# Where the attention half of the even layer's output projection is computed

## The reference, cut to what matters

```python
def attn_delta_mixer(h, pos, w_in, conv_w, a_log, dt_bias, q_gain, k_gain, sinks, gdn_gain, w_out):
    ...
    y_a = sliding_window_attention(partial_rope(q, pos), partial_rope(k, pos), v, sinks)   # (1, 512, 512)
    ...
    o = gated_delta_rule(bq, bk, bv, beta, g)                                              # 4 heads of 128
    o = rms_norm(o, gdn_gain).astype(h.dtype) * jax.nn.silu(bz.reshape(head_shape))
    y_b = o.reshape(bsz, s, GDN_W)
    return jnp.concatenate([y_a, y_b], axis=-1) @ w_out                                    # (1024 -> 1024)

def step(state, inp):            # the recurrence inside gated_delta_rule, one chunk of tokens at a time
    u_c, w_c, a_c, qd_c, kd_c, gl_c = inp
    v_new = u_c - jnp.einsum('bhck,bhkv->bhcv', w_c, state)
    out = jnp.einsum('bhck,bhkv->bhcv', qd_c, state) + jnp.einsum('bhij,bhjv->bhiv', a_c, v_new)
    state = state * gl_c[..., None, None] + jnp.einsum('bhck,bhcv->bhkv', kd_c, v_new)
    return state, out

# layer: x = x + attn_delta_mixer(rms_norm(x), ...);  x = x + hierarchical_moe(rms_norm(x), ...)
```

## Time and profile before

| | |
|---|---|
| median of 3 runs | 1832.97 us (1831.81 to 1833.87) |
| the profiled execution, its own time | 1832.23 us |
| its span | 1830.4 us |
| PE busy | 1754.8 us (96%), 9209 instructions |
| DVE busy | 679.5 us (37%) |
| ACT busy | 452.4 us (25%) |
| POOL busy | 241.1 us (13%) |
| mean granted TensorE clock | 0.981 |

### The profile page before, as it was taken

How to read it: one execution, slowest core, us unless ns; L and a number is a source line. 1 busy time by engine, 2 the same in 40 slices (tenths; PEclk the granted TensorE clock), 3 DMA queues, 4 the chain that set the end, 5 groups by cost and what they waited for, 6 DMA issues and landing times. The chain is left out here.

```text
span 1830.4 us, 23196 instructions
## 1 busy us (share of the span) xinstructions
PE 1754.8 (96%) x9209; PEld 1119.6 (61%) x9209; DVE 679.5 (37%) x1175; ACT 452.4 (25%) x861; POOL 241.1 (13%) x152
## 2 busy tenths in 40 slices
PE   7899787999999999999899999999999999999998
PEld 6678776864454545454578888888745454545453
DVE  3765565342232323332541313141423232323233
ACT  4364534221111111111433232323411111111110
POOL 2531001100000000000334344343100000000000
PEclk9999888999999999999999999999999999999999
DMA  8310020269999999999322312221389999999996
GB/s 190 93 47 4 1 94 1 93 256 410 409 409 410 410 410 410 410 410 409 137 93 69 108 54 92 92 92 47 129 341 409 409 410 410 410 410 410 410 410 248
DMA packets 141176, 460.44 MB, mean 252 GB/s; under 512 B 5552, under 2 KB 31376, under 8 KB 140208
## 3 DMA queue, kind: packets, MB, share of 16 engines
q1 hardware_dynamic: 140368, 457.08, 64.2%
q0 software_dynamic: 736, 2.34, 1.1%
HBM read 457.30 MB, written 2.10 MB: 251 GB/s over the span
## 5 line engine op out<-in xcount | busy, mean ns | idle before, releaser
L1527 PE MATMUL bank<-ring,SCR 128*64 128x512 f32 x2048 | 448.1, 593 | 1.7 <-DVE SCR L1507 0.9
L154 PE MATMUL bank<-ring_r 128*128 128x512 f32 (+1 forms) x1152 | 355.8, 389 | 7.1 <-DVE HT_r L327 4.7
L1527 PEld LDWEIGHTS bank<-ring,SCR 128*64 128x64 f32 x2048 | 152.6, 137 | 290.8 <-issue 286.1
L154 PEld LDWEIGHTS bank<-ring_r 128*128 128x128 f32 x1152 | 217.0, 191 | 52.0 <-issue 4.5
L1965 POOL TENSOR_TENSOR ring_r<-ring,ring_r 128x1024 fp32r<-128x1024 f32 x60 | 147.9, 2500 | 716.2 <-ACT ring_r L1958 716.2
L1538 PE MATMUL bank<-ring,SCR 128*64 128x512 f32 x1024 | 226.8, 595 | 0.0
L1815 DVE TENSOR_TENSOR X<-X,bank 128x512 f32<-128x512 f32 x256 | 164.0, 682 | 99.2 <-PE bank L1545 98.3
L1557 DVE SCALAR_TENSOR_TENSOR SCR<-SCR,bank 128x512 f32<-128x512 f32 x32 | 23.9, 748 | 360.2 <-PE bank L1527 360.2
L1545 PE MATMUL bank<-SCR_r 128*128 128x512 f32 x512 | 151.8, 418 | 3.9 <-DVE SCR_r L1554 3.2
L1538 PEld LDWEIGHTS bank<-ring,SCR 128*64 128x64 f32 x1024 | 70.7, 137 | 132.2 <-issue 128.6
L154 PE MATMUL bank<-ring_r,SCR_r 128*128 128x512 f32 x576 | 137.8, 397 | 2.0 <-DVE X L2202 2.0
(11 more groups left out here) (410 smaller groups left out, 1786.1 us busy)
## 6 DMA issues: line engine op xcount, KB each, us to landing
ring<-in_w_gate_dram SPq DMA_DIRECT2D x64, 2048.0 KB, 15.1
ring<-in_w_up_dram SPq DMA_DIRECT2D x64, 2048.0 KB, 18.4
ring<-in_w_down_dram SPq DMA_DIRECT2D x64, 2048.0 KB, 14.7
ring<-in_w_in_odd_dram SPq DMA_DIRECT2D x8, 2048.0 KB, 8.9
ring<-in_w_in_even_dram SPq DMA_DIRECT2D x16, 512.0 KB, 6.5
ring<-in_w_in_odd_dram SPq DMA_DIRECT2D x8, 1024.0 KB, 8.7
ring<-in_w_out_odd_dram SPq DMA_DIRECT2D x4, 2048.0 KB, 8.0
ring<-in_w_out_even_dram SPq DMA_DIRECT2D x2, 2048.0 KB, 10.3
```

Of the source, the lines that this page charges most:

```text
L154: mm = pe.matmul(out, lhs[a], rhs[b], start=(first and i == 0), stop=(last and i == 2))
L1527: mm = pe.matmul(bank[SLOTS * u:SLOTS * u + SLOTS, :], x_tile(k, u), w[u][:, k, :], start=(k == 0), stop=(k == KT - 1))
```

## The change

The transposes, splits and products of the attention half (g = 0) no longer wait for the delta rule. Six of the eight half tiles, `EARLY = (0, 1, 2, 3, 5, 7)`, get their twelve g = 0 matmuls early and keep their partial sum in a PSUM bank of their own (`out_bank`); the g = 1 matmuls are added later. Half tiles 4 and 6 are made whole, as before.

- In level 5 of the SECOND pair (`lv == LEVELS - 2`) PE transposes attention's tiles 0 and 1, after level 6 tiles 2 and 3. ACT and DVE split them there (`out_upper`, `out_lower`). The transposes of the gates of heads 0 and 1 move from behind `inverse_out` into and behind level 6.
- ACT's `out_squares` of heads 0 and 1 move out of rounds 0 and 1: head 0 goes into level 5, head 1 between `inverse_out` and the last two weight splits. DVE's `gated(0)` moves ahead of round 0, `gated(1)` from round 1 to round 2.
- In each of the four rounds PE gets two pieces of three 128x512 matmuls, one behind `step_in` and one behind `step_out`: half tile 1 in rounds 0 and 1, half tile 3 in rounds 2 and 3.
- Behind the last gate transposes PE computes the g = 0 part of half tiles 0, 2 and 5, then (after `d_y` of all heads) two groups of g = 1 transposes, then the g = 0 part of half tile 7.
- In the projection itself the remaining two g = 1 transpose groups stand behind half tiles 1 and 3. DVE's four `out_lower` of g = 1 all stand ahead of its first residual addition.
- The buffers of the heads are laid out in another order, so that `YTU` and `YTL` are free early; the squares' scratch is `qd` in place of `e_dec`.

```diff
+        def out_bank(n):
+            return PB[n if n < 4 else (4, 5, 4, 7)[n - 4]]
...
+        EARLY = (0, 1, 2, 3, 5, 7)
+        def early_out(pe, n, j):
+            if j == 0:
+                pe.wait_ge(sg("m_tr_d"), {1: 3, 3: 4}.get(n, n // 2 + 1))
+            out_product(pe, n, 0, j, j == 0, False)
...
@@ gdn_pe, levels of SECOND
+                if lv == LEVELS - 2:
+                    pe.wait_ge(sg("d_o_out"), nth(1, NT - 1, NT))
+                    for t in range(2):
+                        out_transposed(pe, 0, t)
+                if lv == LEVELS - 1:
+                    z_transposed(0)
...
+            z_transposed(1)
+            for t in range(2, NT):
+                out_transposed(pe, 0, t)
             each(inverse_out, SECOND)
-            each(z_transposed, FIRST)
             for n in range(NT):
                 each(step_in, SECOND, n)
+                early_out(pe, 1 + n // 2 * 2, 2 * (n % 2))
                 each(step_out, SECOND, n)
+                early_out(pe, 1 + n // 2 * 2, 2 * (n % 2) + 1)
             each(z_transposed, SECOND)
+            for n in (0, 2, 5):
...
+                for j in range(4):
+                    early_out(pe, n, j)
@@ gdn_act
+                if lv == LEVELS - 2:
+                    for t in range(2):
+                        out_upper(act, 0, t)
                 if lv:
                     split_oute_act(act, lv - 1)
+                if lv == LEVELS - 2:
+                    out_squares(0)
+            for t in range(2, NT):
+                out_upper(act, 0, t)
             each(inverse_out, SECOND)
+            out_squares(1)
             split_oute_act(act, 6)
             split_oute_act(act, 7)
             for n in range(NT):
                 each(step_in, SECOND, n)
                 each(step_out, SECOND, n)
-                if n < 2:
-                    out_squares(n)
@@ gdn_dve
+                if lv == LEVELS - 2:
+                    each(no_state, SECOND)
+                    for t in range(2):
+                        out_lower(dve, 0, t)
...
-            each(no_state, SECOND)
+            for t in range(2, NT):
+                out_lower(dve, 0, t)
+            gated(0)
             for n in range(NT):
                 each(step_out, SECOND, n)
-                if n < 2:
-                    gated(n)
+                if n == 2:
+                    gated(1)
@@ oute_pe
             pe.wait_ge(sg("d_y"), GH)
...
+            for t in range(2):
+                out_transposed(pe, 1, t)
+            pe.wait_ge(sg("d_o_out"), nth(3, NT - 1, NT))
+            for j in range(4):
+                early_out(pe, 7, j)
             for n in range(8):
                 t, half = n // 2, n % 2
-                pe.wait_ge(sg("m_tr_d"), 2 * t + 2)
-                if n >= 2:
+                pe.wait_ge(sg("m_tr_d"), 5 + t)
+                if n >= 6:
                     pe.wait_ge(resid, n - 1)
                 router_pe(pe, 0, n)
+                for g in (1,) if n in EARLY else (0, 1):
...
+                if n in (1, 3):
+                    out_transposed(pe, 1, n // 2 + 2)
@@ oute_dve
-            for n in range(8):
+            for t in range(NT):
+                out_lower(dve, 1, t)
             router_gain(dve, 0)
             for n in range(8):
                 dve.wait_ge(sg("m_out"), n + 1)
-                dve.tensor_tensor(xs, xs, PB[4 + n % 2][:, :], ALU.add).then_inc(resid, 1)
+                dve.tensor_tensor(xs, xs, out_bank(n)[:, :], ALU.add).then_inc(resid, 1)
```

More of the change, by code:

```diff
@@ L954, in out_squares @@
                 for t in range(NT):
-                    last = act.activation(H.e_dec[:, t, :], H.og[:, t, :], ACT.Square, accum_out=H.o_ss[:, t:t + 1])
+                    last = act.activation(H.qd[:, t, :], H.og[:, t, :], ACT.Square, accum_out=H.o_ss[:, t:t + 1])
                     if t < NT - 1:
@@ L1171, in gdn_dve @@
             each(gated, SECOND)
-        YTU, YTL = (SCR_r[:, mixed + a:mixed + a + 4096].rearrange("p (k n) -> p k n", k=KT) for a in (0, 4096))
         raw_at = (mixed + 8192, 0)
@@ L1200, in oute_pe @@
                     for j in range(4):
[L1201 to L1204 removed]
+                        mm = out_product(pe, n, g, j, g + j == 0, g == 1 and j == 3)
                 mm.then_inc(sg("m_out"), 1)
+                if n in (1, 3):
+                    out_transposed(pe, 1, n // 2 + 2)
```

56 lines of the change are left out of this document (33 added, 23 removed).

## The result

The changed kernel took 1819.78 us (median of 4 runs, 1817.49 to 1822.34), the kernel before 1832.39 us (4 runs, 1831.52 to 1833.87): ratio 0.9931, 95% interval 0.9919 to 0.9944. It is faster by 12.6 us. The forecast was 9.9. At 1819.78 us it lies 0.3 us inside the faster end of the range that was given, 1819.5 to 1826.5. The profiled execution took 1821.24 us, 11.0 less than that of before.

A forecast was written before the change was run, and what follows sets the result against it. PE, busy 96% of the span, was taken as the bound, with one large hole before the projection. Terms -0.4, -11.9, +1.7 and +0.7 sum to -9.9 us: median 1823.0, range 1819.5 to 1826.5.

The forecast's parts named there:

- Part 1: Levels 5 and 6 to round 0: `inverse_out` 1.6 us late, first product 1.0 earlier, wait about 2.3 for ACT's copy.
- Part 2: The four rounds: 3.64 us for a full round without waits, gate transposes done at 312.7 against 313.1, term -0.4.
- Part 3: Gate transposes to last logits: fewer matmuls and transposes, old wait filled, 3.2 us wait added; 57.4 against 69.3, term -11.9.
- new wait: At half tile 4, PE waits 3.2 us ahead of the router's first transposes for DVE's lower part and residual additions.
- the seams: PE changing between small fp32 and wide products 16 times more, with signal waits: +0.7 us, bounds 0 and 2.
- Part 4: Granted clock: one half-clock fall of some 3.4 us after the 3.2 us wait, costing +1.7; round 0's wait costs 0.
- Part 6: PE's filler behind the last logits, ahead of the count: gain taken as 0, bounds -1.6 and 0.
- rival 3: Experts' first weights land no earlier and eat the earlier start; no change that can be told, 1832; chance 0.04.
- rival 4: Half clock in the mixed work, round 0 to half tile 3: half of it gives 1838, all some 23 us slower; chance 0.04.
- rival 1: Clock falls more often, at round 0's wait, the 3.2 us wait and `inverse_out`: gain 5 to 8, about 1826; chance 0.16.
- rival 2: Clock holds throughout, also behind the logits: gain up to 13.9 us, about 1819.5; chance 0.16.
- the hole of 6.2 us: In the kernel before, PE's wait after the gate transposes at 313.1 us for DVE's last gating; the change was to fill it.

The follow-up runs named there:

- the third set of the same kernel: The changed kernel timed once more without an edit, beside the last variants: 1819.03 us, ratio 0.9926 to the kernel before.
- the second profile: The changed kernel timed again without an edit, beside its first variants: 1819.76 us, ratio 0.9943 to the kernel before.
- the mended kernel: Changed kernel with ACT's round 0 copies ahead of head 1's squares and DVE's last two lower parts behind early residual additions: 1815.93 us, repeated 1814.76.

## Why the prediction came out as it did

The cause it named is the right one, and the experiments isolate it: without the early products the change gains nothing (1834.49), with all of them behind the gate transposes it is at 1825.3, with the pieces in the rounds at 1819. Of this last step the stages give 1.0 us to the pieces; the rest is half clock or lies ahead of level 5, and that the pieces prevent it is not shown. The size was 2.7 us too small by the medians and 1.1 by the profiles; that the median fell inside the range, by 0.3 us, owes something to luck, since the third set of the same kernel has 1819.03, just outside it. Step by step:

**Part 1, levels and round 0.** `inverse_out` was to move from 291.6 to 293.2; it moved to 293.89. DVE's instruction that releases it began at 293.04, where 292.8 had been forecast, and ended at 293.45, and the remaining 0.4 us are on PE, whose eight new transposes start at 292.93, behind level 6's last products and ahead of `inverse_out`. The prediction had allowed 0.3 us for new transposes in level 5 and nothing for those that stand there. It ran at full clock, 1.8 us, as taken. Round 0's first product came at 295.68, forecast 295.0. ACT's first copy: 299.86, forecast 299.3, and ahead of it the squares and two splits that were named. The wait was 1.98 us, forecast 2.3.

```profile
297.98 1.97 ACT L430 CAST ring_r<-ring 128x1024 fp32r<-128x1024 f32 x2
299.86 0.42 ACT L1004 COPY ring<-bank 128x128 f32<-128x128 f32 x2
```

**Part 2, the rounds.** In the third profile of the changed kernel a round takes 3.62 us (301.47 to 305.09), forecast 3.64, with its two pieces and no wait in it. The transposes ended at about 312.9 where the clock held, forecast 312.7. In the profiled execution, with 1.7 us lost to half clock in the rounds, they ended at 314.7.

**Part 3, to the last logits.** No wait at the g = 1 transposes. The last gating ended at 320.5 (319.79 and 0.69 below), where 318 had been forecast; 1.7 of that is the half clock in the rounds. It is hidden under the 36 matmuls, which held PE to 323.2. The new wait was 3.01 us, forecast 3.2, and its parts are those that were named; only the signal to ACT, put at 0.2, took 0.04 us (the transposes end at 339.26, ACT begins at 339.30). DVE's timeline of the changed kernel, against the earlier trace rows:

```profile
293.04 0.41 DVE L1168 TENSOR_SCALAR HT<-bank 64x256 f32<-64x256 f32 x1
...
319.79 0.69 DVE L1192 TENSOR_TENSOR XN<-ring,bank 128x512 f32<-128x512 f32 x1
...
339.91 0.69 DVE L799 TENSOR_TENSOR SCR_r<-bank,SCR_r 128x512 fp32r<-128x512 f32 x1 [5.38 <-ACT SCR_r L794]
340.52 0.45 DVE L1445 TENSOR_TENSOR WR<-WR,gcol 128x288 f32<-128x288 f32 x1
340.89 2.48 DVE L1287 TENSOR_TENSOR X<-X,bank 128x512 f32<-128x512 f32 x4
```

From the end of the gate transposes (314.7) to the last logits (372.6) it was 57.9 us, of which 1.7 is half clock: 56.2 without it. Parts 3 and 5 together had said 57.4 + 0.7 = 58.1. This is the term that was mis-sized, by 1.9. About 1.0 of it is half clock that the kernel before had in its last logits: the 16 products took 2.80 us there and 1.95 now, and the prediction had left that inside the router's 12.7. Another 0.2 is the shorter wait. The remaining 0.7 are mostly the seams, which were put too high: in the second profile, whose clock held, the 168 matmuls take 39.8 us from the start of each group to the next instruction, where 39.4 and 0.7 had been added, and the rounds, where most of the seams lie, are no longer than their parts. The sixteen transposes took 1.9 us, forecast 2.1.

**Part 4, the clock.** One fall behind the new wait and none behind round 0's, +1.7. The profile had one behind each, +3.4; the two later profiles of the same kernel had none, 0. Behind round 0's wait the clock fell in four of the eight profiles that have it, and in none of the five without it. Behind the 3.01 us wait it fell in four of seven, in none of the three that have no wait there and none at the first logits, and not where the filler lay in the wait. (Where the 3.01 us wait had become one of 1.30 us at the logits, the clock fell behind that one, in both profiles.) Eight falls in fifteen, at up to 1.7 us each, make 0.9 us in the mean on top of each wait. What decides in the single case is not shown. Nor is a wait needed: in three of the thirteen profiles with the new order the clock fell in level 6, where PE had been idle for at most 0.56 us at a time. The term for both waits together, 1.7, was right, but as a mean of things that are there or not, and not as one certain fall.

**Part 6, the filler.** It was given 0 with a bound of -1.6; it gained 0.8 (7.6 to 6.8 us) in all three profiles. The count was at 379.39, which is 10.6 earlier: 1.6 later at the gate transposes, -11.4 in parts 3 to 5, -0.8 here. The forecast for the same three was -0.4, -9.5 and 0.

**The experts.** 1440.1 us from the count to the end against 1440.4: they pass the gain on, as forecast, and rival 3 did not come true. Nor did rival 4. By it half clock would have lain in the mixed work of the rounds and half tiles. Apart from the 3.4 us behind round 0's wait, PE is busy for 31.00 of 31 us there at a clock of 1.00, and for 56.00 of 56 in the mended kernel. The Trainium skill ("TensorE: Matmul & The Clock Gate", "A second HAM failure mode: psum-queue depth-cycling") warns of such a case, met with bf16 operands and short idle times between groups of matmuls. Each round here goes through five banks, but without the idle times, so this trace speaks neither for the page nor against it. Between rivals 1 and 2 no choice can be made for the kernel as a whole: the first profile is rival 1 in the two waits, with a larger gain in parts 3 and 6 to set against it, and the other two are near rival 2, 91.8 us to the count, but for a fall in the filler. Their own times, 1818.9 and 1818.0, lie just below that rival's 1819.5. The median lies between.

**Readings that were off.** The prediction says that PE looks full in four stretches; in the first of them, 284 to 286, it was busy for 1.56 of 2.00 us. And it takes the half clock around the hole of 6.2 us as two falls that cost 3.4. The list of granted clocks has 315.7 to 322.5 at 0.50, but PE waited until 319.36, so that only 1.6 us were lost. Rival 1's three terms, added in full, leave a gain of 4.6 and not of 5.

**Where the gain came from.** In the stretch of the table PE was idle for 13.7 us before and for 6.7 in every profile of the changed kernel; half clock cost 8.2 us before and 5.1 or 1.7 in the changed kernel. So 7.0 us are shorter waits, and 3.1 to 6.5 are clock that was not lost; 0.3 to 0.5 are left for the work itself. Only 1.6 us of the 8.2 lay behind the hole. The others were in `inverse_out`, behind the wait of 3.35 us, and at and behind the last logits. The forecast had both, but in one number.

**What stays open.** Why the kernel without pieces has medians 5.5 and 6.4 us above those of the changed one, where its stages account for 4.0 and 4.2. Its granted clocks, 0.980 and 0.979 in the mean of its executions against 0.982 to 0.984, point to half clock; where it lies in the executions without a profile, and why there is more of it, they do not say. And what moves the start of level 5.

## What to carry to other kernels

When PE waits for a chain over three engines, shortening the work ahead of the chain only moves the wait; put PE work that does not hang on the chain behind its last input, and count two gains, the waits and the clock; here they were 7.0 and 3.1 to 6.5 us, and most of the second did not lie behind the hole. Then look at each queue past which the moved steps go: here ACT's squares ahead of a 0.27 us copy and DVE's lower parts ahead of the first residual additions made two new waits, and mending the order of both queues gave another 4 us. Read such edits by stages of the trace between fixed instructions; the medians alone would have called three of them useless.

## What the hardware showed that was not expected

The same kernel, in the same stretch, with the same waits to 0.01 us, lost 5.1 us to half clock in one profile and 1.7 in two. Waits of 1.97 to 3.01 us inside busy work were followed by a fall in 8 of 15 cases. A wait of 1.30 us at the first logits was followed by 6.8 us of half clock in one profile (350.0 to 356.8) and by 3.4 in the other (348.0 to 351.4). A stretch whose order no kernel changed, up to level 5, ended anywhere from 283.5 to 288.2 us, and the clock was at 0.50 for 41 to 51 us of it.
